# Six other byte offsets for the features of a two-block network kernel

## The reference

```
for l in range(DEPTH):                       # DEPTH = 2
    x = layer_norm(ALPHA * x + 0.5 * swiglu(x, ffn_w1[l, 0], ffn_w2[l, 0]), ...)
    mix = hybrid_mixer(x, w_in[l], ...)      # x @ w_in: 1024 x 7168
    x = layer_norm(ALPHA * x + mix, ...)
    x = layer_norm(ALPHA * x + 0.5 * swiglu(x, ffn_w1[l, 1], ffn_w2[l, 1]), ...)
```

## Time and profile before

| | us |
|---|---|
| median of the two runs shown | 2158.36 (2154.62 and 2162.1) |
| the profiled execution, its own time | 2158.29 |
| its span, first to last instruction | 2156.5 |
| PE busy in the span | 2128.5 |
| PEld busy | 1931.4 |
| DVE busy | 1429.7 |
| ACT busy | 902.0 |

### The profile page before, as it was taken

The page is one execution under the profiler, slowest core; times in us unless marked ns, Lnnn a source line. Parts: engine busy times, 40 slices in busy tenths (PEclk is TensorE's granted clock), DMA queues, the critical chain, the costliest instruction groups (busy, mean ns, idle before and its releaser), DMA issues.

```text
span 2156.5 us, 35429 instructions
## 1 busy us (share of the span) xinstructions
PE 2128.5 (99%) x14996; PEld 1931.4 (90%) x14996; DVE 1429.7 (66%) x2066; ACT 902.0 (42%) x1066; POOL 18.7 (1%) x36
## 2 busy tenths in 40 slices
PE   9999999999999999999999999999999999999998
PEld 8998999999989989999899768888788889999996
DVE  4556878676566548876756777887666457665665
ACT  4334456343343334374434352222344344443442
POOL 0000000000000000000000000000000000000000
PEclk9999999999999999999999999999999999999999
DMA  9655555666566555555575422222112232332331
GB/s 346 227 187 196 196 196 205 230 250 251 189 256 242 196 195 196 196 188 212 207 238 209 178 96 79 79 79 78 66 53 79 88 117 79 118 118 79 118 118 59
DMA packets 29005, 349.56 MB, mean 162 GB/s; under 512 B 2992, under 2 KB 5424, under 8 KB 8368
## 3 DMA queue, kind: packets, MB, share of 16 engines
q1 hardware_dynamic: 24672, 313.42, 39.5%
q0 software_dynamic: 4176, 33.89, 4.1%
HBM read 346.24 MB, written 1.05 MB: 161 GB/s over the span
## 4 chain that ended last, share of the span: by engine, by line
PE 94%; DVE 3%; ACT 2%; DVEq 1%; issue 1%; ACTq 0%
PE banks L922 13%; PE banks L780 12%; PE banks L775 12%; PE banks L776 12%; PE banks L1009 8%; PE banks L1084 6%; PE banks L1083 6%; PE banks L1087 6%; PE banks L792 3%; PE banks L1097 2%; PE banks L1101 2%; PE banks L1098 2%; PE banks L1279 2%; PE banks L1278 2%; PE banks L1280 2%; PE banks L878 1%
## 5 line engine op out<-in xcount | busy, mean ns | idle before, releaser
L2112 DVE TENSOR_TENSOR w_lo<-ring,w_hi 128x2048 fp32r<-128x2048 f32 x290 | 662.0, 2290 | 393.1 <-ACT w_hi L1523 388.7
L1523 ACT ACTIVATE w_hi<-ring 128x2048 fp32r<-128x2048 f32 x290 | 555.8, 1917 | 677.3 <-PE banks L780 449.2
L775 PE MATMUL banks<-x_hi,w_hi 128*128 128x256 f32 x2112 | 496.9, 278 | 0.5 <-ACT w_hi L1523 0.5
L776 PE MATMUL banks<-x_lo,w_hi 128*128 128x256 f32 x2112 | 495.7, 277 | 0.0
L775 PEld LDWEIGHTS banks<-x_hi,w_hi 128*128 128x128 f32 x2112 | 397.2, 188 | 1.5 <-issue 1.5
L776 PEld LDWEIGHTS banks<-x_lo,w_hi 128*128 128x128 f32 x2112 | 397.2, 188 | 0.0
L780 PE MATMUL banks<-x_hi,w_lo 128*128 128x256 f32 x2112 | 284.6, 277 | 1.0 <-DVE w_lo L2112 1.0
L780 PEld LDWEIGHTS banks<-x_hi,w_lo 128*128 128x128 f32 x2112 | 260.7, 188 | 1.4 <-DVE w_lo L2112 1.4
L1083 PE MATMUL banks<-x_hi,w_hi 128*128 128x512 f32 (+1 forms) x656 | 233.1, 368 | 0.0
L1084 PE MATMUL banks<-x_lo,w_hi 128*128 128x512 f32 (+1 forms) x656 | 226.7, 359 | 0.0
L1560 ACT ACTIVATE arena<-banks 128x512 f32<-128x512 f32 (+5 forms) x178 | 79.7, 471 | 286.8 <-PE banks L1087 167.4
(11 more groups left out here) (378 smaller groups left out, 2812.9 us busy)
## 6 DMA issues: line engine op xcount, KB each, us to landing
ring<-weights SPq DMA_DIRECT2D x147, 2048.0 KB, 7.7
arena<-mods POOLq DMA_DIRECT2D x11, 2048.0 KB, 11.5
bcast<-lnrows POOLq DMA_DIRECT2D x12, 512.0 KB, 4.9
ring<-weights SPq DMA_DIRECT2D x2, 1024.0 KB, 10.0
filt_sb<-filt POOLq DMA_DIRECT2D x2, 609.0 KB, 20.9
xrow<-x SPq DMA_DIRECT2D x1, 1024.0 KB, 5.2
arena<-hy_consts POOLq DMA_DIRECT2D x1, 1024.0 KB, 11.5
xrow<-ctx_rows POOLq DMA_DIRECT2D x1, 1024.0 KB, 6.6
```

What stands on the lines that cost most here:

```text
L775: nc.tensor.matmul(out, hi[:, k, t * P:(t + 1) * P], x_h[:, k, :], start=k == 0, stop=False)
L776: nc.tensor.matmul(out, hi[:, k, t * P:(t + 1) * P], x_l[:, k, :], start=False, stop=False)
L1523: nc.scalar.activation(hi, raw, ACT.Copy).then_inc(w_hi_done, 1)
L2112: v.tensor_tensor(lo, raw, hi.bitcast(F32), ALU.subtract).then_inc(w_lo_done, 1)
```

## The change

Each of the six stages gets its own pair of tiles, `x_his[n]` and `x_los[n]`, in the same two regions of memory. Each region is 512 bytes longer, and the stage's tile begins 128, 192, 96, 288, 224 or 160 bytes past the region's start. The region of `x_lo` starts where it did, 448 past the grid. That of `x_hi` starts 8704 bytes later, 17 times 512, so also 448 past. The tiles of stages 0 to 5 therefore begin 64, 128, 32, 224, 160 and 96 bytes past a grid point, hi and lo alike. `arena` begins 1024 bytes later than before and keeps its 448. It is 1024 bytes shorter, and `mod_at` is counted from its end with 256 elements in place of 512. The number, order and kind of all instructions stay, and so do the waits.

```diff
+X_SHIFTS = (128, 192, 96, 288, 224, 160)
...
         xt_at = at[0]
-        x_lo = place("x_lo", [P, KT, SEQ], F32R)
-        x_hi = place("x_hi", [P, KT, SEQ], F32R)
+        lo_at, hi_at = xt_at, xt_at + 4 * KT * SEQ + 512
+        at[0] = hi_at + 4 * KT * SEQ + 512
+        x_his = [place(f"x_hi{n}", [P, KT, SEQ], F32R, hi_at + shift) for n, shift in enumerate(X_SHIFTS)]
+        x_los = [place(f"x_lo{n}", [P, KT, SEQ], F32R, lo_at + shift) for n, shift in enumerate(X_SHIFTS)]
...
-        mod_at = (SBUF_END - arena_at) // 32 * 8 - 512
+        mod_at = (SBUF_END - arena_at) // 32 * 8 - 256
...
-                    pair(l, x_hi, x_lo, "up", f, j, split=None if j else l * 3 + 2 * f)
+                    pair(l, x_his[3 * l + 2 * f], x_los[3 * l + 2 * f], "up", f, j, split=None if j else l * 3 + 2 * f)
...
                 turn(l, 0)
+                x_hi, x_lo = x_his[3 * l + 1], x_los[3 * l + 1]
...
             def features_hi(l, n):
+                x_hi = x_his[0 if l is None else 3 * l + n + 1]
...
             def features_lo(l, n, split):
+                x_hi, x_lo = x_his[split], x_los[split]
```

## The result

The changed kernel takes 2181.86 us (median of 2 runs, 2181.37 and 2182.35). The kernel before takes 2158.36, and the ratio is 1.0112 with a 95% interval of 1.0078 to 1.0147. The forecast was 2185 us. The profiled executions took 2158.29 and 2182.35 us, which is 24.1 us apart.

A forecast was written before the change was run, and what follows sets the result against it. PE, busy 99% of the span, was taken as the bound. The stages' and first pairs' added matmul times sum to +26.7 us on 2158.36, giving a forecast of 2185 us, 1.2% more, range 2150 to 2206.

The forecast's parts named there:

- The bound and what can move: PE alone sets the time; only the pace of 6912 matmuls in the six stages can change.
- Stage 0: Distance 64, first network stage: from a mean of 115.1 to 117.8 ns a matmul, +2.6 us.
- Stage 1: Distance 128: 2.2% more, as in the 512-column rows, from 113.3 to 115.8 ns, +3.1 us.
- Stages 2 to 5: Distances 32, 224, 160, 96: 119 ns each; +5.5 us for stages 2 and 3, +7.1 and +1.2 for 4 and 5.
- Rival two: Weight load and moving stream meet in memory, slower by over 2%, typically 2202 to 2230 us; chance 0.14.
- The first pairs: First matmul pairs of the stages, 576 matmuls: 3 ns more each, +1.7 us.
- Rival one: The offset does nothing, each stage lands on one of two paces; likely 2151 to 2173 us, chance 0.34.
- Its half about the levels: Part of Rival one: interruptions decide which of two paces, 113.3 or 117.8 ns, a stage runs at.
- Its second way: Way for Rival two to pass 2%: four stages off multiples of 64, some 4400 matmuls, cost 9.8 ns more.
- Rival three: Some distances are free of the addition, a stage at 109 ns; typically 2125 to 2151 us, chance 0.07.
- The rule against the change: The skill's separate read ports on TensorE: offsets would not matter, 109.2 ns a step estimated, time stays at 2158 us.

The follow-up runs named there:

- the scan: Three runs of the changed kernel's layout with the six stages at other distances, 352 in the first: 2181.00, 2186.67 and 2196.13 us, against the kernel before.

## Why the prediction was right, point by point

**The bound and what can move.** Right. PE's pace is the time. The matmuls that stream x_hi and x_lo hold 23.9 of the 24.1 us, with -1.6 us ahead of the second block and 1.7 us in it beside them, and putting the shifts to 0 gives it all back (1.0002).

**Stage 0, taken from the rows with weights moving 64 past the features.** The value was right, 117.8 measured. The reason was partly luck: those rows show both levels, and features moving at 64 or 320 showed only 117.8, in three stages of three kernels.

**Stage 1, taken from the 512-column rows.** The size was off, +7.3 us measured for +3.1. The step that failed is taking the price of rows 5 as a share. Their 2.2% does not carry over to 256 columns, where distance 128 costs 5.4 to 6.6 ns, 4.8 to 5.8%. Taken in ns the same rows have 5.0 ns a matmul and would have given 118.3, or +6.2 us.

**Stages 2 to 5, taken at 119 from the gate weights.** The row at 352 was read rightly. In the scan 352 gave 120.0, and stage 5 at 96, the same modulo 256, gave 120.0. It was wrong to see a class of "no multiples of 64" in it: 32, 160 and 224 give 116.9, 117.4 and 118.3, 0.7 to 2.1 ns under the 119. Together stages 2 to 4 were sized at 18.1 us and cost 12.8, stage 5 at 1.2 and cost 2.1. Rival two counted "some 4400" matmuls in these four stages. They are 4128 outside the first pairs and 4512 with them, which makes its 9.8 ns 9.6 to 10.5.

**The first pairs.** Sized at +1.7, they came out at -0.8 us. Of that, 1.2 us is the very first one: it took 11.4 us in place of 12.6, because the granted clock from 14 to 17 us was already 1.00 there in the execution profiled after and 0.50 in the one before.

So 26.7 came near 23.9 us because errors cancel: stage 1 was 4.2 us too little and stage 5 0.9, stages 2 to 4 were 5.3 us too much and the first pairs 2.5. That the total was this close is luck. The mechanism, a price for each distance read from other operands, was right, and the law behind it was not yet known.

**The rivals.** Rival one, that the offset does nothing, is out: five of six paces are neither 113.3 nor 117.8, and they follow the distance into other stages. Its half about the levels is right. They exist at 448 and 192, 4.5 ns apart, and 1.1 to 1.4 ns apart at 32, 128 and 160, and they change at interruptions. The 17 runs of the kernel before spread from 2148.9 to 2165.0 us. Levels can make such a spread, since 6336 matmuls at 4.5 ns are 28.5 us (an estimate), but no kernel here has two profiles, so it is not shown that they do. Rival two was not met by this change. Its second way, many matmuls a few ns slower, was the real danger: 452 in all six stages gave a ratio of 1.0216. Its picture of one catastrophic distance is not borne out, since the worst was 121.1. Rival three is out for the distances tried: none was below 113.3.

**The rule against the change.** By the Trainium skill ("TensorE: Matmul & The Clock Gate", section "Step-by-step: what each phase is for") loading the next weights takes nothing from the running matmul. For float32r with 256 columns no run here bears out that offsets do not matter. The step is 113.3 to 121.1 ns by the distance of the two operands and the level, and the estimate of 109.2 from its figure was not reached at any distance. The transposes that the prediction took for an agreement are none: the figure is for N columns at 2.4 GHz, and their 109 ns for 128 columns are nearly twice what it gives there.

**What stays open.** That the weight load and the moving stream meet in memory fits a law of the distance, with a period of 256 bytes, that vanishes at the half clock. No row shows such a meeting, so it is argued and not shown. Open are also what the two levels are, why the mixture of two distances costs what it does, and why weights moving at 64 show the lower level and features moving at 64 do not.

## What to carry to other kernels

A PE that is busy 99% can still run its matmuls 7% slower than it might (121.1 ns against 113.3 here): count matmuls in a stretch that holds one kind, and compare with other operands of the same shape. When float32r matmuls with 256 columns and a weight load each fill the time, place the moving tile 192 bytes past the start of the stationary tile modulo 256, exactly (shown here for weight tiles of 512 bytes and feature tiles of 1024), and measure again after any tile between them changes its size. Before two versions are compared, look at how far runs of one version spread, and which stages of each profile were at which level.

## What the runs showed of the hardware that was not expected

The step of a float32r matmul with 256 moving columns and a load of 128 columns depends on the distance of its two operands modulo 256 bytes: 113.3 ns at 192, 119.7 at 188, 121.1 at 196, 116.7 to 116.9 at 32, and 117.4 to 120.0 at the other multiples of 32. The absolute address did not matter (96 bytes more for all: 113.3 and 117.8 again). The best place has a second level of 117.8, entered and left at a short interruption (other products, two small transposes among them, or a wait). At 32, 128 and 160 there are two levels as well, 1.1 to 1.4 ns apart. At the half clock the step was 213 to 214 ns at 448, 444, 384, 192 and 0. With 512 columns the steps were 228.9 to 233.4 ns.
